# The second block's attention taken by pairs of heads: what a different order and grouping of the same products does

## What is computed

```python
def hybrid_mixer(x, ...):
    proj = x @ w_in
    y_a = rwkv7_mixer(...)
    q, k, v = jnp.split(proj[..., OFF_MOBA:OFF_SSM], 3, axis=-1)
    y_b = moba_attention(heads(q), heads(k), heads(v))
    y_c = s5_mixer(...)
    gates = jax.nn.sigmoid(proj[..., OFF_GATE:] + gate_b).reshape(Bsz, L, N_BRANCHES, D_MODEL)
    merged = (gates[..., 0, :] * (y_a @ w_up_rwkv)
              + gates[..., 1, :] * (y_b @ w_up_moba)
              + gates[..., 2, :] * (y_c @ w_up_ssm))
    return merged @ w_out
```

## Time and profile before

| | us |
|---|---|
| median of 3 runs | 1383.82 |
| the 3 runs | 1383.82, 1384.68, 1379.47 |
| the profiled execution, device time | 1379.36 |
| its span, first to last instruction | 1377.6 |
| of it TensorE busy with matmuls | 1180.9 (86%) |
| VectorE busy | 412.0 (30%) |
| ScalarE busy | 206.9 (15%) |
| mean share of TensorE's full clock granted | 0.948 |

### The profile page before, as it was taken

The page is one execution under the profiler, slowest core; times in us unless marked ns, Lnnn a source line. Parts: engine busy times, 40 slices in busy tenths (PEclk is TensorE's granted clock), DMA queues, the critical chain, the costliest instruction groups (busy, mean ns, idle before and its releaser), DMA issues.

```text
span 1377.6 us, 18774 instructions
## 1 busy us (share of the span) xinstructions
PE 1180.9 (86%) x8146; PEld 642.3 (47%) x8146; DVE 412.0 (30%) x812; ACT 206.9 (15%) x389; POOL 121.4 (9%) x148
## 2 busy tenths in 40 slices
PE   6989997986667767666999999999799879999996
PEld 5745455532222222222545547888676443333332
DVE  4265733110001001000256385422464331111113
ACT  3112421010000000000000031111321132112111
POOL 0010000000005870000044200000000000000000
PEclk9999998998889789888999999999999989999999
DMA  8432739999999999999714431312313629999991
GB/s 290 162 110 75 305 124 400 430 427 425 428 428 425 428 429 426 426 430 423 291 31 157 164 137 62 123 36 91 122 61 127 283 87 408 423 421 422 421 422 73
DMA packets 62397, 377.31 MB, mean 274 GB/s; under 512 B 6129, under 2 KB 7537, under 8 KB 37105
## 3 DMA queue, kind: packets, MB, share of 16 engines
q1 hardware_dynamic: 60736, 369.64, 65.9%
q10 hardware_dynamic: 1584, 6.55, 1.3%
HBM read 375.13 MB, written 1.05 MB: 273 GB/s over the span
## 4 chain that ended last, share of the span: by engine, by line
PE 61%; DMA 30%; DVE 5%; ACT 2%; issue 1%; POOL 0%; SPq 0%; DVEq 0%; ACTq 0%
DMA arena<-in_w_expert_up 22%; PE psum L468 10%; PE psum L471 9%; PE psum L2636 6%; DMA arena<-in_expert_w_up 5%; PE psum L1298 3%; PE psum L2144 3%; PE psum L763 3%; PE psum L2660 3%; DMA arena<-in_w_expert_gate 3%; PE psum L2247 2%; PE psum L2671 2%; PE psum L1904 2%; PE psum L1010 2%; PE psum L1328 2%; PE psum L1092 1%
## 5 line engine op out<-in xcount | busy, mean ns | idle before, releaser
L1298 PE MATMUL psum<-arena 128*32 128x256 f32 x2048 | 151.0, 445 | 95.1 <-DMA arena<-in_w_expert_up 56.8
L468 PE MATMUL psum<-arena 128*128 128x512 f32 x352 | 160.1, 604 | 2.9 <-ACT arena L507 1.6
L1298 PEld LDWEIGHTS psum<-arena 128*32 128x32 f32 x2048 | 70.7, 124 | 176.7 <-DMA arena<-in_w_expert_up 73.4
L1328 PE MATMUL psum<-arena 128*32 128x512 f32 x512 | 123.9, 635 | 15.6 <-DMA arena<-in_w_expert_down 10.3
L471 PE MATMUL psum<-arena 128*128 128x256 f32 x544 | 123.6, 382 | 3.0 <-ACT arena L1732 2.0
L2636 PE MATMUL psum<-arena 128*64 128x512 f32 x512 | 116.0, 595 | 2.1 <-DMA arena<-in_expert_w_up 2.1
L471 PEld LDWEIGHTS psum<-arena 128*128 128x128 f32 x544 | 101.4, 189 | 20.2 <-issue 5.6
L468 PEld LDWEIGHTS psum<-arena 128*128 128x128 f32 x352 | 65.0, 191 | 81.6 <-issue 81.3
L1328 PEld LDWEIGHTS psum<-arena 128*32 128x32 f32 x512 | 31.4, 116 | 95.8 <-issue 69.9
L1359 DVE TENSOR_TENSOR arena<-arena,psum 128x256 f32<-128x256 f32 x16 | 6.8, 422 | 224.0 <-ACT arena L1342 224.0
L2636 PEld LDWEIGHTS psum<-arena 128*64 128x64 f32 x512 | 35.8, 137 | 69.3 <-issue 68.9
(11 more groups left out here) (464 smaller groups left out, 1285.7 us busy)
## 6 DMA issues: line engine op xcount, KB each, us to landing
arena<-in_w_expert_gate SPq DMA_DIRECT2D x32, 2048.0 KB, 25.3
arena<-in_w_expert_up SPq DMA_DIRECT2D x32, 2048.0 KB, 26.3
arena<-in_w_expert_down SPq DMA_DIRECT2D x31, 2048.0 KB, 24.4
arena<-in_w_in SPq DMA_DIRECT2D x21, 2048.0 KB, 8.8
arena<-in_expert_w_gate SPq DMA_DIRECT2D x32, 1024.0 KB, 11.5
arena<-in_expert_w_up SPq DMA_DIRECT2D x32, 1024.0 KB, 13.6
arena<-in_expert_w_down SPq DMA_DIRECT2D x32, 1024.0 KB, 10.2
arena<-in_w_out SPq DMA_DIRECT2D x4, 2048.0 KB, 8.0
```

The costliest lines, as they stand in the source:

```text
L468: mm = pe.matmul(o, lhs[:, k, sub * P:(sub + 1) * P], w[:, k, :], start=(k == 0), stop=(k == kt - 1))
L1298: mm = pe.matmul(ps[32 * c:32 * c + 32], xin[:, e, k], w[:, j, 256 * n:256 * n + 256], start=(k == 0), stop=(k == KD - 1))
L1328: mm = pe.matmul(y_ps[at:at + 32, 512 * n:512 * n + 512], hid_T4[:, j, half], w[:, j, 512 * n:512 * n + 512], start=(half == 0 and j == 0) ...
```

## The change

A new function, `attention_by_pairs`, takes the place of `attention` for the second block (the first block keeps `attention`).

- Scores: `scores(p)` does the four matmuls of heads 2p and 2p + 1, alternating between row halves and between banks 4 and 5.
- Sums over v: `weigh(p)` does the four matmuls of the pair, alternating between column halves, with one signal for the pair.
- Transposes: `turn(p)` does both heads, into banks 6 and 0.
- Buffers: four `sc` and four `pT` instead of two each.
- Orders: TensorE's and VectorE's strings are new, and `scores(1)` (heads 2 and 3) stands before the first `turn`. One half job of merge for RWKV's branch now stands behind the attention's last piece.
- Merge's third branch waits for three pairs' output, and for the fourth only ahead of its fourth matmul.

ScalarE's string is as before; its pieces are now of two heads.

```diff
+            def tensor(pe):
...
+                def scores(p):
+                    if p >= 1:
+                        pe.wait_ge(*count(tag + "_biased", 2 * p))
+                    for t in range(NT):
+                        for e in range(2):
+                            r = slice(64 * e, 64 * e + 64)
+                            mm = pe.matmul(bank(4 + e)[:, t * SEQ:(t + 1) * SEQ], qkT[r, p, t * P:(t + 1) * P],
+                                           qkT[r, 4 + p, :], start=True, stop=True)
+                            if t == NT - 1:
+                                mm.then_inc(inc(tag + "_scores"), 1)
+
+                def turn(p):
...
+                    for h in (2 * p, 2 * p + 1):
+                        pe.wait_ge(*count(tag + "_probs", h + 1))
+                        if h >= 2:
+                            pe.wait_ge(*count(tag + "_probsT", h - 1))
+                        for t in range(NT):
+                            for k in range(NT):
+                                mm = pe.transpose(bank((6, 0)[h % 2])[:, k * SEQ + t * P:k * SEQ + (t + 1) * P],
+                                                  sc[h % 4][:, t, k * P:(k + 1) * P], ident)
+                        mm.then_inc(inc(tag + "_probs_turned"), 1)
+
+                def weigh(p):
+                    pe.wait_ge(*count(tag + "_probsT", 2 * p + 2))
+                    for k in range(NT):
+                        for e in range(2):
+                            h = 2 * p + e
+                            mm = pe.matmul(weighed(p)[64 * e:64 * e + 64], src[:, k, 2 * HW + h * HD:2 * HW + (h + 1) * HD],
+                                           pT[h % 4][:, k], start=(k == 0), stop=(k == NT - 1))
+                    mm.then_inc(inc(tag + "_weighed"), 1)
+
+                scores(0)
+                yield
+                scores(1)
+                yield
+                for p in range(PAIRS):
+                    turn(p)
+                    yield
+                    weigh(p)
+                    if p + 2 < PAIRS:
+                        scores(p + 2)
+                    yield
...
+                def bias(h):
+                    dve.wait_ge(*count(tag + "_scores", h + 1))
+                    if h >= 4:
+                        dve.wait_ge(*count(tag + "_probs_turned", h - 3))
...
-            branches = ((2, ycT, ("glu_out", 1)), (0, yaT, ("rw_out", 2)), (1, ybT, ("mb_out", 4)))
+            branches = ((2, ycT, ("glu_out", 1)), (0, yaT, ("rw_out", 2)), (1, ybT, ("mb_out", 3)))
...
+                            if place == 2 and d == 0 and k == 3:
+                                pe.wait_ge(*count("mb_out", 4))
...
-            take_turns(pe, "gr" + "ggr" + "g" * 7 + "r" + "ggr" + "gr" * 6 + "r" + "gr" + "grrgr" * 3 + "gggggg" + "t" + "mm" + "t" + "r" + "tm" * 14,
+            take_turns(pe, "gr" + "ggr" + "g" * 7 + "r" + "ggr" + "gr" * 6 + "r" + "gr" + "grrgr" * 3 + "gggggg" + "t" + "mm" + "t" + "r" + "mmtm" + "tmtmm" * 3 + "tmt",
...
-            take_turns(dve, "mt" + "tm" * 7 + "t", m=merged.parts[1], t=attention2.parts[1])
+            take_turns(dve, "mt" * 7, m=merged.parts[1], t=attention2.parts[1])
```

More of the change, by code:

```diff
@@ L2121, in two_blocks, with attention_by_pairs, weighed, vector @@
         ybT = cols.take("ybT", 1024).rearrange("p (c s) -> p c s", c=4)
-        attention2 = attention("mb", qkv2, proj_qkv2.done, ybT, const("causal").rearrange("p (t s) -> p t s", t=NT), False,
-                               banks_free=[("rw_y", NCH), *proj_gates_tail.done], out_banks=(7, 1), second_free=[("rw_out", 2)],
-                               qkT=rwkv7.y.rearrange("p q c w s -> p (q c w s)").rearrange("p (c s) -> p c s", s=SEQ))
+        def attention_by_pairs(tag, src, inputs_done, out, mask, qkT, banks_free, out_banks, second_free):
+            sc, pT = ([cols.take(f"{tag}{n}{j}", 512).rearrange("p (t s) -> p t s", t=NT) for j in range(4)]
+                      for n in ("sc", "pT"))
+            den, rden, nmax = tiny(2 * HEADS), tiny(2 * HEADS), tiny(2 * HEADS)
+            PAIRS = HEADS // 2
+            def weighed(p):
+                return bank(out_banks[p % 2])[:, (p // 2) * SEQ:(p // 2 + 1) * SEQ]
+            def tensor(pe):
+                pe.wait_ge(*count("const_loaded", 32))
+                for sem, n in (*inputs_done, *banks_free):
+                    pe.wait_ge(*count(sem, n))
+                for j in range(4):
+                    for c in (2 * j, 2 * j + 1):
+                        for t in range(NT):
+                            mm = pe.transpose(bank(4 + j)[:, (c % 2) * SEQ + t * P:(c % 2) * SEQ + (t + 1) * P],
+                                              src[:, t, c * P:(c + 1) * P], ident)
+                    mm.then_inc(inc(tag + "_turned"), 1)
+                yield
+                pe.wait_ge(*count(tag + "_T", 4))
+                def scores(p):
[9 more added lines that the diff above has]
+                def turn(p):
+                    if p == 0:
+                        for sem, n in second_free:
+                            pe.wait_ge(*count(sem, n))
+                    for h in (2 * p, 2 * p + 1):
+                        pe.wait_ge(*count(tag + "_probs", h + 1))
+                        if h >= 2:
+                            pe.wait_ge(*count(tag + "_probsT", h - 1))
+                        for t in range(NT):
+                            for k in range(NT):
[20 more added lines that the diff above has]
+                        scores(p + 2)
+                    yield
+            def vector(dve):
+                step = vchain(dve)
+                def bias(h):
+                    dve.wait_ge(*count(tag + "_scores", h + 1))
+                    if h >= 4:
+                        dve.wait_ge(*count(tag + "_probs_turned", h - 3))
+                    s = sc[h % 4]
+                    dve.scalar_tensor_tensor(s, dist, -2.0 ** -(h + 1), bank(4 + h % 2).rearrange("p (t s) -> p t s", t=NT),
+                                             ALU.mult, ALU.add).then_inc(inc(tag + "_biased"), 1)
+                    dve.wait_ge(*count(tag + "_biased", h + 1))
+                    step(dve.tensor_tensor(s, s, mask, ALU.add))
+                    dve.tensor_reduce(nmax[:, 2 * h:2 * h + 2], s, AXX, ALU.max, negate=True)\
+                       .then_inc(inc(tag + "_max"), 1)
+                def divide(h):
+                    dve.wait_ge(*count(tag + "_exp", h + 1))
+                    step(dve.reciprocal(rden[:, 2 * h:2 * h + 2], den[:, 2 * h:2 * h + 2]))
+                    dve.tensor_tensor(sc[h % 4], sc[h % 4], along(rden[:, 2 * h:2 * h + 2], SEQ, 2), ALU.mult)\
+                       .then_inc(inc(tag + "_probs"), 1)
+                def take_out(p):
+                    dve.wait_ge(*count(tag + "_weighed", p + 1))
+                    dve.tensor_copy(out[:, p], weighed(p)).then_inc(inc(tag + "_out"), 1)
+                bias(0)
+                bias(1)
+                divide(0)
+                divide(1)
+                yield
+                bias(2)
+                bias(3)
+                yield
+                divide(2)
+                divide(3)
+                take_out(0)
+                bias(4)
+                bias(5)
+                yield
+                divide(4)
+                divide(5)
+                take_out(1)
+                yield
+                bias(6)
+                bias(7)
+                yield
+                divide(6)
+                divide(7)
+                take_out(2)
+                yield
+                take_out(3)
+            def scalar(act):
+                for j in range(4):
+                    act.wait_ge(*count(tag + "_turned", j + 1))
+                    act.activation(qkT[:, 2 * j:2 * j + 2], bank(4 + j).rearrange("p (e s) -> p e s", e=2), ACT.Copy,
+                                   scale=HD ** -0.5 if j < 2 else 1.0).then_inc(inc(tag + "_T"), 1)
+                yield
+                for p in range(PAIRS + 1):
+                    if p:
+                        for h in (2 * p - 2, 2 * p - 1):
+                            act.wait_ge(*count(tag + "_probs_turned", h + 1))
+                            if h >= 4:
+                                act.wait_ge(*count(tag + "_weighed", h // 2 - 1))
+                            act.activation(pT[h % 4].rearrange("p t s -> p (t s)"), bank((6, 0)[h % 2]), ACT.Copy)\
+                               .then_inc(inc(tag + "_probsT"), 1)
+                    if p < PAIRS:
+                        for h in (2 * p, 2 * p + 1):
+                            act.wait_ge(*count(tag + "_max", h + 1))
+                            for t in range(NT):
+                                ins = act.activation(sc[h % 4][:, t], sc[h % 4][:, t], ACT.Exp,
+                                                     bias=nmax[:, 2 * h + t:2 * h + t + 1],
+                                                     accum_out=den[:, 2 * h + t:2 * h + t + 1])
+                            ins.then_inc(inc(tag + "_exp"), 1)
+                    yield
```

(2 more changed lines are left out.)

4 lines of the change are left out of this document (added).

## The result

| | us |
|---|---|
| median before, 6 runs | 1381.40 (1379.05 to 1384.68) |
| median after, 6 runs | 1368.55 (1366.47 to 1369.88) |
| ratio, 95% interval | 0.9905 (0.9889 to 0.9921) |
| a second timing of the same two kernels | 1381.99 (9 runs), 1365.28 (5 runs) |
| its ratio, interval | 0.9878 (0.9859 to 0.9897) |

The kernel became faster by 0.95%, 12.9 us between the medians; a second timing gave 1.22%, 16.7 us. The forecast was 1369, with a range of 1362 to 1375.

A forecast was written before the change was run, and what follows sets the result against it. The prediction took TensorE to bound the stage; gains of 3.15 + 3.88 + 4.1 + 1.64 + 1.25 + 0.4 = 14.4 us, taken from the 1383.8 us median, gave 1369, range 1362 to 1375.

The forecast's parts named there:

- (a): Attention scores: a pair in two row halves costs 1.07 us, about one head's time; gain 3.15 us.
- (b): Sums over v: a pair in two column halves overlaps and takes 1.05 us; gain 3.88 us.
- rival 1: Sums over v: column halves don't overlap, 3.9 us of gain missing, time 1373; chance 0.08.
- (c): Stage's beginning: TensorE's wait for VectorE's division before the first transposes of probabilities is filled; gain 4.1 us.
- (d): After the wait at the beginning: TensorE's clock no longer falls, half job and sums run at full speed; gain 1.64 us.
- (e): Stage's end: merge work covers the waits of 0.7 and 0.56 us around the last sums and output copy; gain 1.25 us.
- (f): Merge's half jobs: three fewer stand behind attention products of another shape; gain some 0.4 us, ends 0 and 0.6.
- What is late next: Attention pairs: VectorE is next to be late, but no wait arises, with 0.5 us to spare at the tightest.
- Rival 3: Behind the stage: block 2's expert loads keep their own time and lose the gain, 1380; chance 0.07.
- Rival 4: Softmax of a pair: a longer chain makes TensorE wait and the kernel slower, 1395; chance 0.04.

The follow-up runs named there:

- no_alternation: Changed kernel with the even head's matmuls issued ahead of the odd head's, in scores and sums; first scores to out projection 53.45 us against 53.40.
- same_cols: Changed kernel with both heads' sums over v in one column half, head by head; first scores to out projection 56.82 us against 53.40.
- wait_back: Changed kernel with TensorE's order altered: second pair's scores and first transposes ahead of three merge half jobs; first scores to out projection 59.28 us against 53.40.
- vector_plus1: Changed kernel with the mask added twice per head, one more VectorE operation each; first scores to out projection 56.52 us against 53.40.
- heads_filled: Kernel before, only TensorE's order changed: three merge half jobs before the first turn; first scores to out projection 72.54 us against 68.45.

## Why the prediction was right

- The forecast of 14.4 us for the stage met 15.05 in the trace, and 1369 met 1368.55. The second agreement is closer than it deserves. The forecast took 14.4 from 1383.8, the median of three runs of the kernel before. Over six runs that median is 1381.40, 2.4 less, and the medians differ by 12.9, 1.5 less than forecast; the two errors nearly cancel. A second timing of the changed kernel gave 1365.28, still within the range.
- (a) Scores: 1.07 a pair forecast, 1.06 found. The forecast rested on a row of before that already contained the case, and its remark that alternation adds nothing was shown by no_alternation.
- (b) Sums over v: 1.05 taken between 0.86 and 2.02, 1.01 found. The gain is 4.0 against 3.9. That 3.4 of it is the overlap was shown by same_cols. The experts' rows were the right neighbours, and rival 1 is out. So is the rule that the prediction set beside it, by which (b) would have brought nothing: a pair in the same rows and different column halves takes 1.01 us, against 1.87 in one column half.
- (c), (d) The wait and the clock: both gone from the trace. RWKV's transposes and the wait behind them took 5.09 us on the chain of before and take 1.02 now, so (c) is 4.07 against 4.1. For (d) the prediction counted a half job and the sums, 1.64, and left out the first transposes, which stand in the earlier trace rows with 0.66 against 0.44 at full clock. With them it is 1.86. The 5.9 us of wait_back are no measure of the two, as said there.
- (e) The end: the waits of 0.7 and 0.56 are gone, as forecast. A half job behind each of the last two pieces covers them.
- (f) Changes of shape: the mis-sized term. From the first scores on, merge's 176 records add up on the chain to 40.73 us before and to 39.00 after. Less the 1.11 that (d) already has, this is 0.62, where I took 0.4 with 0.6 as its end. I had priced three changes at 0.15 each, though the two rows named beside it, 1.92 and 1.73, differ by 0.19. The transposes of probabilities went from 3.75 to 4 x 0.87 = 3.48, which is 0.27, of which 0.22 is the clock of the first group, above. These two oversights, 0.2 in each of (d) and (f), and the 0.16 that (b) brought beyond its 3.88 make up most of what separates 15.05 from 14.4.
- "What is late next": the prediction left head 6 a margin of 1.0 us and head 7 one of 0.5, the tightest. In the trace the divisions of these heads end at 1026.21 and 1027.01. Head 6's four transposes begin at 1027.38 and head 7's half a group later, at 1027.82. The margins are 1.2 and 0.8, a little wider than forecast and in the forecast place:

```profile
1025.52 0.69 DVE L2210 TENSOR_TENSOR arena<-arena 128x512 f32<-128x512 f32 x1
1026.32 0.69 DVE L2210 TENSOR_TENSOR arena<-arena 128x512 f32<-128x512 f32 x1
1026.93 0.42 DVE L2215 COPY arena<-psum 128x256 f32<-128x256 f32 x1
1027.38 1.04 PE L2167 MATMUL psum<-arena 128*128 128x128 f32 x8
```

- Rival 3 (later parts do not follow): they follow. The next experts' first load (start us, us, what) is issued right behind merge's last addition, as in the earlier trace rows,

```profile
1048.38 0.34 SPq L2725 DMA_DIRECT2D arena<-in_expert_w_gate  x1
```

  and the stretch from the experts to the end takes 252.1 to 252.6 against 252.8. What the forecast left out is that the clock can fall at another place in a later stage: 1.0 us went in the router's part.
- Rival 4 (slower) needed a chain of a pair much longer than found. In vector_plus1, the nearest that was run, eight more operations cost 3.1 us. A chain as long as the rival's was not run.

## What to carry to other kernels

When TensorE has no wait in a stage, look for products that use half of its rows or columns and put two of them, in different halves, next to each other: here each such pair cost what one head had cost. Order and overlap should be priced apart, for half of this gain was order and could be had without pairs. Here that took new orders on both engines together; the one attempt with TensorE's order alone was 4.1 us slower. When the overlap shortens TensorE's part, the next engine's margin shrinks with it, so work the stage forward with that engine before adding anything.

## What the runs showed of the hardware that I had not expected

- Products in different halves overlap whatever the order of issue within the pair: 1.02 and 1.07 us for eight records issued head by head, 1.01 and 1.06 when alternated.
- A group of products in a half has about 0.2 us of its time once, however many products it holds: a pair in one and the same half takes 1.92 and 1.87 us, not 2.12 and 2.02. The change of shape around the group is my reading of it, not shown.
- The length of a wait doesn't tell how long the clock stays low. The wait of 4.1 us before had 3.4 us at 1.2 GHz with it. Waits of 1.9 and 1.0 us with a pair of scores between them (wait_back) had 6.9 us. In heads_filled one wait of 2.8 us, up to 1005.99, had 3.4 us with it, and one of 2.65 us, up to 1017.04, had 6.9 us (0.74 over 6.5 us and 0.51 over 7; columns as in the earlier trace rows):

```profile
1003.00:1009.50 6.50, 3.68 (x10) 2.81 (x10) 2.66 (x4) 0.00 (x0) 0.00 (x0) 0.74 0.00 0
1016.00:1023.00 7.00, 5.96 (x13) 3.65 (x14) 1.76 (x4) 1.09 (x4) 0.00 (x0) 0.51 0.50 168
```
